# The sample columns of a causal depthwise convolution: one instruction a tap, or products over overlapping stretches and a sum

## The reference, cut to what matters

```python
glu = a * jax.nn.sigmoid(b)
# prompt
glu_hist = jnp.concatenate([jnp.zeros((bsz, CONV_WIDTH - 1, D_CONV), glu.dtype), glu], axis=1)
# sample
glu_hist = jnp.concatenate([state_conv.astype(glu.dtype), glu], axis=1)

y = lax.conv_general_dilated(glu_hist, w_dw[:, None, :], window_strides=(1,), padding='VALID',
                             dimension_numbers=('NWC', 'WIO', 'NWC'),
                             feature_group_count=D_CONV) + b_dw
y = jax.nn.silu(layernorm(y, conv_ln_g, conv_ln_b))
return y @ w_conv_out + b_conv_out
```

## Time and profile before

| | us |
|---|---|
| median of three timed runs | 1753.26 |
| profiled execution, its own time | 1749.72 |
| its span in the trace | 1748.1 |
| PE busy | 1331.3 (76%) |
| DVE busy | 1140.4 (65%) |
| ACT busy | 636.5 (36%) |
| POOL busy | 243.6 (14%) |

### The profile page before, as it was taken

How to read it: one execution, slowest core, us unless ns; L and a number is a source line. 1 busy time by engine, 2 the same in 40 slices (tenths; PEclk the granted TensorE clock), 3 DMA queues, 4 the chain that set the end, 5 groups by cost and what they waited for, 6 DMA issues and landing times. The chain is left out here.

```text
span 1748.1 us, 26217 instructions
## 1 busy us (share of the span) xinstructions
PE 1331.3 (76%) x8642; PEld 794.3 (45%) x8642; DVE 1140.4 (65%) x1498; ACT 636.5 (36%) x912; POOL 243.6 (14%) x262
## 2 busy tenths in 40 slices
PE   3578887774459999796996987989930787789785
PEld 2245555553336556464653644545510343344342
DVE  5356666664328999999997574533351677777774
ACT  5234444444221111110110362421100567667763
POOL 0110000003000000000000000001004343223322
PEclk9978999997569999898997998999965799999998
DMA  6500000002122222122211005433313798889984
GB/s 233 139 8 1 0 0 0 0 6 53 7 87 60 67 68 67 38 67 80 56 57 57 1 16 184 165 111 134 128 53 110 264 329 311 312 316 330 323 322 98
DMA packets 48612, 203.61 MB, mean 116 GB/s; under 512 B 11744, under 2 KB 12992, under 8 KB 35984
## 3 DMA queue, kind: packets, MB, share of 16 engines
q1 hardware_dynamic: 29904, 156.91, 25.4%
q0 software_dynamic: 16352, 37.15, 8.1%
q10 hardware_dynamic: 2304, 8.95, 2.0%
HBM read 180.63 MB, written 40.00 MB: 126 GB/s over the span
## 5 line engine op out<-in xcount | busy, mean ns | idle before, releaser
L1101 DVE SCALAR_TENSOR_TENSOR big<-c_region,c_taps,big 128x1024 f32 x240 | 308.1, 1284 | 0.0
L1952 DVE SCALAR_TENSOR_TENSOR xnT<-e_gu,xnT 128x2048 f16<-128x2048 f32 x64 | 146.6, 2291 | 104.4 <-ACT xnT L1884 104.4
L1884 ACT ACTIVATE xnT<-e_gu 128x2048 f16<-128x2048 f32 x64 | 122.2, 1911 | 142.5 <-DMA e_gu<-w_gu 142.4
L67 PE MATMUL c_psb<-xnT,c_w_h 128*128 128x364 f16 x456 | 145.8, 320 | 16.9 <-DVE c_w_l L1069 16.9
L68 PE MATMUL c_psb<-xnT,c_w_h 128*128 128x364 f16 x456 | 145.8, 320 | 0.0
L69 PE MATMUL c_psb<-xnT,c_w_l 128*128 128x364 f16 x456 | 145.7, 320 | 0.0
L67 PE MATMUL c_psa<-xnT,c_w_h 128*128 128x364 f16 x312 | 102.0, 327 | 33.0 <-DVE c_gate_b L1075 33.0
L67 PE MATMUL e_psG<-xnT,e_xT_h 128*128 128x512 f16 x256 | 102.9, 402 | 3.4 <-issue 3.4
L68 PE MATMUL e_psG<-xnT,e_xT_h 128*128 128x512 f16 x256 | 102.7, 401 | 0.0
L69 PE MATMUL e_psG<-xnT,e_xT_l 128*128 128x512 f16 x256 | 102.4, 400 | 0.0
L68 PE MATMUL c_psa<-xnT,c_w_h 128*128 128x364 f16 x312 | 101.7, 326 | 0.0
(11 more groups left out here) (321 smaller groups left out, 3279.1 us busy)
## 6 DMA issues: line engine op xcount, KB each, us to landing
e_gu<-w_gu SPq DMA_DIRECT2D x64, 1024.0 KB, 11.3
big<-w_dn SPq DMA_DIRECT2D x32, 1024.0 KB, 8.5
c_w<-w_feat SPq DMA_DIRECT2D x40, 512.0 KB, 3.7
m_gates<-gates POOLq DMA_DIRECT2D x8, 1092.0 KB, 5.8
qkv<-w_in SPq DMA_DIRECT2D x8, 768.0 KB, 4.3
n_x<-x_all SPq DMA_DIRECT2D x9, 512.0 KB, 4.7
o_x<-x_all SPq DMA_DIRECT2D x9, 512.0 KB, 4.0
y_all<-h SPq DMA_DIRECT2D x9, 512.0 KB, 2.9
```

The source lines that it names most:

```text
L67: pe.matmul(out, stat[0], mov[0], start=start, stop=False)
L1101: dve.scalar_tensor_tensor(y_p, glu[:, p, j:j + SEQ], tap, y_p, op0=ALU.mult, op1=ALU.add).then_inc(tap_done, 1)
L1884: act.activation(gu_h[:, p, halves[half]], gu32[:, p, halves[half]], ACT.Copy, scale=S_W).then_inc(gu_high[half], 1)
L1952: dve.scalar_tensor_tensor(gu_l[:, p, halves[half]], gu32[:, p, halves[half]], S_W, gu_h[:, p, halves[half]], op0=ALU.mult, op1=ALU.subtra ...
```

## The change

The prompt columns stay one instruction a tap. The sample columns are computed four sequences at a time (SEQS = 4, so i = 0 and 1 below), by two kinds of instruction. `sample_terms(i)` multiplies, for 4 sequences, 8 outputs and 31 taps, the value at position output + tap (`spread`: an access pattern whose last two dimensions both step by one element, so that neighbouring stretches overlap) by the tap's weight (the same 31 for each of the 32 outputs). The 992 products go into the prompt columns of the other slot of `glu`, whose convolution is over. `sample_sum(i)` sums them over the taps into 4 x 8 columns of y. After both, one instruction adds the bias to the 64 columns. These five stand behind taps 3, 6, 13, 16 and 24 of the prompt's chain and count on a semaphore of their own, `smp_done`.

```diff
-        tap_done = sem("c_tap")
+        tap_done, smp_done = sem("c_tap"), sem("c_smp")
...
-        NTAP = 2 * TAPS
+        SEQS = NSEQ // 2
...
-                dve.tensor_scalar(y_s, seqs[:, :, 0:DSEQ], taps[:, ds(k, 1), 0:1].rearrange("p a b -> p (a b)"),
-                                  vecs[:, 0, ds(k, 1)], ALU.mult, ALU.add).then_inc(tap_done, 1)
+
+                def spread(i):
+
+                    a = seqs[:, i * SEQS:(i + 1) * SEQS, 0:DSEQ]
+                    return bass.AP(tensor=a.tensor, offset=a.offset, ap=list(a.ap) + [[1, TAPS]])
+
+                weights = taps[:, ds(k, 1), :].unsqueeze(1).to_broadcast([P, SEQS, DSEQ, TAPS])
+                terms = glu[:, 1 - p, HIST:HIST + SEQS * DSEQ * TAPS].rearrange("p (b i j) -> p b i j", b=SEQS, i=DSEQ)
+
+                def sample_terms(i):
+                    dve.wait_ge(smp_done, 5 * k + 2 * i)
+                    dve.tensor_tensor(terms, spread(i), weights, ALU.mult).then_inc(smp_done, 1)
+
+                def sample_sum(i):
+                    dve.wait_ge(smp_done, 5 * k + 2 * i + 1)
+                    dve.tensor_reduce(y_s[:, i * SEQS:(i + 1) * SEQS], terms, AX.X, ALU.add).then_inc(smp_done, 1)
+
                 for j in range(1, TAPS):
                     tap = taps[:, ds(k, 1), j:j + 1].rearrange("p a b -> p (a b)")
-                    dve.wait_ge(tap_done, NTAP * k + 2 * j - 1)
+                    dve.wait_ge(tap_done, TAPS * k + j)
                     dve.scalar_tensor_tensor(y_p, glu[:, p, j:j + SEQ], tap, y_p, op0=ALU.mult,
                                              op1=ALU.add).then_inc(tap_done, 1)
-                    dve.wait_ge(tap_done, NTAP * k + 2 * j)
-                    dve.scalar_tensor_tensor(y_s, seqs[:, :, j:j + DSEQ], tap, y_s, op0=ALU.mult,
-                                             op1=ALU.add).then_inc(tap_done, 1)
+                    if j in (3, 13):
+                        sample_terms(j // 10)
+                    if j in (6, 16):
+                        sample_sum(j // 10)
+                    if j == 24:
+                        dve.wait_ge(smp_done, 5 * k + 4)
+                        dve.tensor_scalar(row(y, k)[:, SEQ:T], row(y, k)[:, SEQ:T], vecs[:, 0, ds(k, 1)], None,
+                                          ALU.add).then_inc(smp_done, 1)
                     if j == 11:
                         low(4 * k + 6, 2)
...
-                dve.wait_ge(tap_done, NTAP * k + NTAP)
+                dve.wait_ge(tap_done, TAPS * k + TAPS)
+                dve.wait_ge(smp_done, 5 * k + 5)
                 dve.sem_inc(glu_free, 1)
...
-            pe.wait_ge(tap_done, NTAP * KC)
+            pe.wait_ge(tap_done, TAPS * KC)
+            pe.wait_ge(smp_done, 5 * KC)
```

## The result

The changed kernel takes 1763.28 us (median of 5 runs, 1759.86 to 1764.01) against 1753.26: ratio 1.0056, interval 1.0040 to 1.0073. A second measurement on another occasion gave 1764.89 against 1751.32, ratio 1.0074 (1.0053 to 1.0096). The direction was forecast, the size was not: 23.4 us and a range of 1767 to 1788 were predicted, 10 to 14 came.

A forecast was written before the change was run, and what follows sets the result against it. DVE's tap loop was taken to bound the convolution stage, so added time moves the end one for one. Terms of 1.76 + 1.76 - 0.50 - 0.10 = 2.92 us a chunk, x 8 = 23.4, gave 1776.7 us, range 1767 to 1788.

The forecast's parts named there:

- the seven items: The numbered terms for one of 8 chunks in DVE's tap loop, summing to 2.92 us longer a chunk.
- What else moves: Passage on effects outside the sum: PE waits longer at the odd chunk's gate but does not become the bound.
- A: Rival, plain taps: removed instructions give back their distance, tap to tap 1.21 us, 16 us faster, 1737; chance 5%.
- B: Rival, plain taps: address work moves ahead of the wait, tap to tap 1.33 us, 1758.6; chance 8%.
- C: Rival, products and sums: short overlapping runs are slow, 0.70 us more each, 1799 (sums alone 1788); chance 7%.
- Item 1: Plain taps and tap 0: removing 30 L1104 and one L1096 a chunk gains 0, hidden by the prompt chain's wait.
- the rule weighed in the prediction: The skill's claim for DVE: a semaphore after each operation costs nothing extra, so minimise the count of operations.
- Item 2: Behind taps 11, 20 and 18 of odd chunks: L1104 does cost 0.20 us each, gain 0.50 a chunk.
- Items 3 and 4: Two products and two sums of 992 elements in each chunk's taps: 0.88 us each, 1.76 per pair.
- Item 5: Bias add on 64 elements behind tap 24: takes L1104's place in the gap, costs 0, at most 0.03 us.
- Item 6: End of the chunk, last L1104 gone before L1082: 0.10 us gained, bounds 0 and 0.20.
- PE's wait at the gate: PE waiting for DVE at the odd chunk's gate: to grow from 13 to 19 us.

The follow-up runs named there:

- a3: The changed kernel with two semaphore increments of the sequencer before each tap, loop body 376 instructions instead of 256: 1771.49 us, ratio 1.0105.
- a5: The kernel before with 100 semaphore increments in front of the loop, the body unchanged: 1745.91 us, ratio 0.9967.
- d3: The kernel before with 100 increments ahead of the loop, measured again: 1747.10 us, ratio 0.9972.
- d1: The kernel before with 125 semaphore increments in front of the loop, the body unchanged: 1752.93 us, ratio 1.0007.
- a1: The kernel before without its 240 L1104 instructions (samples keep tap 0 only, outputs incomplete): 1737.07 us, ratio 0.9922.
- b3: The changed kernel with the prompt's taps in two sums, even and odd, added at the chunk's end: 1728.37 us, ratio 0.9875.
- b2: The changed kernel with DVE's loop over pairs of chunks written out, so addresses and wait values are constants: 1741.61 us, ratio 0.9943.

## Why the prediction was wrong: right about the chain, blind to the branch

The step that failed is the reading of the row "issue", 10.4 us, as "one for each return of the loop over pairs of chunks". The prediction had the row, gave it the right place, and carried it over unchanged: neither the seven items nor "What else moves" holds a term for the return, so it stood at nothing without a reason. It was a cost of the body's length and place, and the change shortened the body from 354 to 256 instructions. The missing term is 3 x (2.88 - 0.28) = 7.8 us at the branches, and by the chunks a little more: odd chunks with a return were 54.26 on average and are 54.16, where 2.68 more was due, so 3 x 2.78 = 8.3. a3 puts that term back and gets 1771. a5 takes it from the kernel before and gets 6.3 us (its repetition d3 4.2, the stretch 7.1); d1, with 25 instructions more ahead of the loop, has the stall again. "After the taps all is unchanged and shifted" held: 803.3 us before and 802.3 after. None of the three rivals named the return; A was refuted by a1, B and C by the changed kernel's own rows.

The other steps, in their order:
- Item 1, L1104 free in a plain tap: right. Period 1.43 with it, 1.42 without. The 0.01 goes with address work that became shorter (46 ns where 57 stood; a1 has both too, so it isn't the products' doing); it gives 22.5 x 0.01 x 8 = 2 us that the sum didn't have. Against the rule weighed in the prediction, a wait for the forerunner does cost (1.20 from start to start in b3, 1.32 in b2, 1.42 here), and 240 instructions less gained 7.0 us in a1's chunks, 0.03 each. The Trainium skill, VectorE: DVE Perf Modes, has the advice to minimise the count of operations in its section Rules for kernel authors.
- Item 2, 0.20 behind each L1069: right. From the tap before to the tap after it 2.53 before, 2.34 after.
- Items 3 and 4, 1.18 and 1.19 us, 0.88 each in the period: measured 1185 and 1179 ns, 2.30 to 2.31 between the taps around them. No surcharge for overlapping stretches of 31 elements, or for sums over them.
- Item 5, the bias add: nothing, as forecast.
- Item 6, 0.10 at the chunk's end: last tap's start to L1082 was 1.89, is 1.77.
- PE's wait at the gate: it was to grow from 13 to 19 us, with two chunks' 5.8. The longest was 13.7 and is 16.2, because the loop's period grew by 2.6 only. PE didn't become the bound; its first matmul of the mean starts at 959.95, where 968.6 was named.
- The sum for a chunk: 2.92 forecast, 2.68 measured; 21.4 for eight. This part of the forecast holds, and with the 8.3 taken off it is 13.1. The trace has 13.0, the medians 10.0 and 13.6 on two occasions.
- DVE's busy time: 3 us less forecast, 3.7 less measured. DVE's busy time said nothing here about what its work cost.

How I could have seen it: the row said "issue", 3 times, 3.6 us at most, on an engine that waits for nobody. The earlier trace rows show that the return within a pair, without a branch, costs 0.41. The page has the packets of the instruction queue, 30 of them. Those three facts priced the stall at about 3 us a return, and the change takes (354 - 256) / 2 = 49 instructions out of each chunk. They didn't say at which length the stall goes. A bound "if the shorter body returns without it, minus 8 to 9" would have put the range's lower end at 1767 - 9 and included the result.

## What to carry to other kernels

A small instruction between two links of a dependent chain can be free: price it by the distance between starts, with and without it, and look for what the next link waits for (its wait, and the address computation behind the wait) before paying to remove it. The better edit here was to break the chain (two sums, 1.43 to 1.20 a tap) and only then replace the small instructions; the same replacement lost 2.7 us a chunk before that and gained 1.4 after it, in this kernel, where a long instruction lasts 1.28 us and a small one 0.28. And count the instructions of a loop's body whenever an edit lengthens or shortens it: unexplained idle time at a loop's return is a price that moves with the body's length, and with how many instructions stand ahead of the loop.

## What the runs showed of the hardware that was not expected

- A returning loop of 354 instructions on DVE stalls 2.7 to 3.1 us at the branch, one of 234 to 298 doesn't (0.3). With 354 it depends on the place: 100 instructions ahead of the loop remove the stall, 0, 80 and 125 don't. Fetches of 8192 bytes come some 128 instructions apart (123 to 132 of the trace).
- In a chain of taps of 1.28 us, a wait followed by a computed address costs 0.14 us behind the end of the instruction waited for (period 1.42), a wait with constant addresses 0.04 (1.32); not to wait lets the next one start 0.08 before the recorded end (1.20).
- 992 products from a pattern that reads each value up to 8 times, stretches of 31 elements one apart, run at the rate of a broadcast product without such a pattern: 1185 ns for 992, against 1216 for 1024. The sum over the innermost 31 takes 1179, against 1220 for a sum over 1024.
